# Output projection of a hybrid decoder layer: 512-column chunks of two k-tiles, three matmuls per stationary block

## The reference

```
h = h + jnp.einsum('btd,de->bte', merged, w_out[layer])
return rmsnorm(h, final_norm_w)
```

## Time and profile before

| | |
|---|---|
| median of three runs | 2974.49 us (2974.31 to 2974.5) |
| span of the profiled execution | 2972.4 us; the page states no other time for it |
| TensorE matmul, weight load | busy 2954.2 and 2585.2 us |
| VectorE, ScalarE | busy 1700.5 and 1311.9 us |
| DMA | 552.28 MB, 186 GB/s, hardware queue at 59.9% of 16 engines |
| granted TensorE clock | 0.999 on average |

### The profile page before, as it was taken

The page is one execution under the profiler, slowest core; times in us unless marked ns, Lnnn a source line. Parts: engine busy times, 40 slices in busy tenths (PEclk is TensorE's granted clock), DMA queues, the critical chain, the costliest instruction groups (busy, mean ns, idle before and its releaser), DMA issues.

```text
span 2972.4 us, 46667 instructions
## 1 busy us (share of the span) xinstructions
PE 2954.2 (99%) x17061; PEld 2585.2 (87%) x17061; DVE 1700.5 (57%) x1973; ACT 1311.9 (44%) x1526; POOL 6.9 (0%) x23
## 2 busy tenths in 40 slices
PE   9999999999999999999999999999999999999998
PEld 7888888888888888888888888888888888888887
DVE  7666666666665555555555555555555555555555
ACT  6444444444444444444444444444444444444444
POOL 0000000000000000000000000000000000000000
PEclk9999999999999999999999999999999999999999
DMA  7555555555556555555566666666666666666665
GB/s 242 178 177 168 170 174 174 171 171 169 174 169 190 187 185 184 182 188 188 186 187 185 185 188 184 185 184 188 185 185 187 184 185 188 184 207 205 207 206 193
DMA packets 550941, 552.28 MB, mean 186 GB/s; under 512 B 17217, under 2 KB 547826, under 8 KB 550898
## 3 DMA queue, kind: packets, MB, share of 16 engines
q1 hardware_dynamic: 550898, 551.71, 59.9%
HBM read 547.45 MB, written 4.19 MB: 186 GB/s over the span
## 4 chain that ended last, share of the span: by engine, by line
PE 99%; DMA 0%; DVE 0%; ACT 0%; ACTq 0%; SPq 0%; issue 0%; DVEq 0%
PE PS L833 64%; PE PS L828 33%; PE SC L874 1%; DMA XS<-in_x 0%; PE SS L874 0%; PE OB L883 0%; PE OB L884 0%; PE SC L864 0%; PE OB L882 0%; PE SS L889 0%; PE PS L819 0%; PE SC L819 0%; PE OB L819 0%; DVE WS L481 0%; ACT U L327 0%; ACT H L453 0%
## 5 line engine op out<-in xcount | busy, mean ns | idle before, releaser
L833 PE MATMUL PS<-U,WS 128*128 128x512 f32 x5632 | 1982.3, 396 | 0.0
L481 DVE TENSOR_TENSOR WS<-RAW,WS 128x1024 fp32r<-128x1024 f32 x1024 | 1249.4, 1225 | 1177.2 <-ACT WS L309 1146.2
L309 ACT ACTIVATE WS<-RAW 128x1024 fp32r<-128x1024 f32 x1024 | 1084.0, 1060 | 1591.9 <-PE PS L833 1589.2
L828 PE MATMUL PS<-U,WS 128*128 128x256 f32 x5632 | 1574.7, 282 | 0.5 <-DVE WS L481 0.5
L833 PEld LDWEIGHTS PS<-U,WS 128*128 128x128 f32 x5632 | 1053.3, 188 | 245.0
L828 PEld LDWEIGHTS PS<-U,WS 128*128 128x128 f32 x5632 | 1061.8, 189 | 8.8 <-issue 0.8
L833 PE MATMUL PS<-WS,U 128*128 128x512 f32 x1536 | 533.5, 390 | 0.0
L828 PE MATMUL PS<-WS,U 128*128 128x256 f32 x1536 | 430.8, 283 | 0.0
L833 PE MATMUL PS<-Y,WS 128*128 128x512 f32 x1024 | 361.7, 397 | 0.0
L833 PEld LDWEIGHTS PS<-WS,U 128*128 128x128 f32 x1536 | 287.3, 188 | 58.3
L828 PEld LDWEIGHTS PS<-WS,U 128*128 128x128 f32 x1536 | 290.1, 189 | 2.6
(11 more groups left out here) (161 smaller groups left out, 631.9 us busy)
## 6 DMA issues: line engine op xcount, KB each, us to landing
RAW<-in_w_in SPq DMA_DIRECT2D x768, 512.0 KB, 3.7
RAW<-in_w_out SPq DMA_DIRECT2D x128, 512.0 KB, 3.8
RAW<-in_w_branch_a SPq DMA_DIRECT2D x64, 512.0 KB, 3.7
RAW<-in_w_branch_b SPq DMA_DIRECT2D x64, 512.0 KB, 3.8
XS<-in_x SPq DMA_DIRECT2D x8, 512.0 KB, 9.5
XR<-in_x SPq DMA_DIRECT2D x16, 256.0 KB, 4.0
out_dram<-H SPq DMA_DIRECT2D x8, 512.0 KB, 4.2
FW<-in_final_norm_w SPq DMA_DIRECT2D x16, 128.0 KB, 3.8
```

The costliest lines, as they stand in the source:

```text
L309: act.activation(WS[s][:, :, 0:GW], RAW[s][:, :, :], ACT.Copy).then_inc(hi_ready, 1)
L481: dve.tensor_tensor(WS[s][:, :, GW:2 * GW], RAW[s][:, :, :], WS[s][:, :, 0:GW], ALU.subtract).then_inc(lo_ready, 1)
L828: return pe.matmul(bank[:, T:2 * T], stat_lo, both[:, 0:T], start=False, stop=stop, skip_group_check=True)
L833: op = pe.matmul(bank, stat_hi, both, start=first, stop=last, skip_group_check=True)
```

## The change

The output projection is cut into eight groups of 512 output columns. A chunk is still 512 KB and still fills one ring slot, but holds two k-tiles of 512 columns (`wide` is the view of the same tile). A group has sixteen chunks. For each k-tile and each half of the positions there are three matmuls of 512 columns into one bank: high x high, high x low and low x high, all three onto the same columns. The bank then holds the finished sum, so that the copy to `SM` and the addition that joined two halves of a bank go. VectorE adds the residual straight from PSUM, over [128, 2, 512], and multiplies by the gain; ScalarE squares 512 columns per half. `GA` and `GB` become two halves of one tile `HG`, which holds the group's `h`. The loads of `XR` and `FW` are twice as wide and half as many. The last four chunks of the merge stage prefill the ring with the first chunks of the output projection, so they use the wide view too.

```diff
+OW = 2 * GW
+CO = 2 * CD
+NO = D // OW
-TURNS_OUT = 2 * CD // RING
+TURNS_OUT = 2 * CO // RING
...
+        def wide(tile):
+            return tile[:, :, :].rearrange("p (k h) c -> p k (h c)", h=2)
...
-            with sp.Fori(0, NG // 2) as i:
+            with sp.Fori(0, NO // 2) as i:
                 for n in range(2):
-                    col = column(i * 2 + n, 0)
-                    for c in range(CD):
-                        load(w_out[0], c, col, OUT_TURN + TURNS_OUT * i + (n * CD + c) // RING, c % RING)
+                    cols = bass.ds((i * 2 + n + 1) * OW - OW, OW)
+                    for c in range(CO):
+                        s = c % RING
+                        src = w_out[0][c * 2 * P:(c + 1) * 2 * P, cols]
+                        sp.wait_ge(lo_ready, RING * (OUT_TURN + TURNS_OUT * i + (n * CO + c) // RING) + s - (RING - 1))
+                        sp.dma_start(wide(RAW[s]), src.rearrange("(k p) c -> p k c", p=P)).then_inc(raw_loaded[s], 16)
...
-                    small_half(OUT_GROUP + 2 * i + n, RING * (OUT_TURN + TURNS_OUT * i) + CD * (n + 1), n)
-                    act.wait_ge(h_ready, 2 * i + n + 1)
+                    act.wait_ge(drained, OUT_GROUP + 2 * i + n + 1)
                     for b in range(2):
-                        act.activation(SM[n][:, b, :], (GA, GB)[n][:, b * T:(b + 1) * T], ACT.Square,
+                        act.activation(SM[b][:, :, :], pair(HG[:, b, :]), ACT.Square,
                                        accum_out=SSQ[:, b, bass.ds(i * 2 + n, 1)]).then_inc(h_sq, 1)
...
-                    drain_group(h, OUT_GROUP + 2 * i + n, n)
-                    dve.tensor_tensor(h, h, XR[:, :, cols], ALU.add).then_inc(h_ready, 1)
+                    dve.wait_ge(w_used, RING * (OUT_TURN + TURNS_OUT * i) + CO * (n + 1))
+                    dve.wait_ge(xr_loaded[n], i * 32 + 32)
+                    if not (first and n == 0):
+                        dve.wait_ge(h_sq, 4 * i + 2 * n)
+                    dve.tensor_tensor(HG[:, :, :], PS[n][:, :, :], XR[:, :, cols], ALU.add).then_inc(drained, 1)
...
-                dve.tensor_tensor(small, PS[1][:, b, T:2 * T], XR[:, b, cols], ALU.add)
-                dve.tensor_tensor(h, PS[1][:, b, 0:T], small, ALU.add)
+                dve.tensor_tensor(h, PS[1][:, b, :], XR[:, b, cols], ALU.add)
...
+            def wide_chunk(par, c, halves=(0, 1)):
+                w = wide(WS[c % RING])
+                for k in range(2):
+                    at_k = 2 * c + k
+                    for b in halves:
+                        top, low = U[:, at_k, b * P:(b + 1) * P], U[:, at_k, T + b * P:T + (b + 1) * P]
+                        bank = PS[par][:, b, :]
+                        pe.matmul(bank, top, w[:, k, 0:OW], start=at_k == 0, stop=False)
+                        pe.matmul(bank, top, w[:, k, OW:2 * OW], start=False, stop=False)
+                        op = pe.matmul(bank, low, w[:, k, 0:OW], start=False, stop=at_k == KT - 1)
+                return op
...
+            for c in range(CO - RING):
+                pe.wait_ge(lo_ready, chunk0 + c + 1)
+                wide_chunk(1, c).then_inc(w_used, 1)
             for b in range(2):
-                for c in range(CD):
+                for c in range(CO - RING, CO):
```

More of the change, by code:

```diff
@@ L397, in merge @@
                 for c in range(2 * CD + 2 * CB):
-                    hi(turn + c // RING, c % RING)
+                    hi(turn + c // RING, c % RING, is_wide=last and c >= 2 * CD + 2 * CB - RING)
                     if c in (CD + 2, 2 * CD + 2):
@@ L430, in output @@
                 for n in range(2):
-                    for c in range(CD if not (last and n == 1) else RING):
-                        hi(OUT_TURN + TURNS_OUT * i + (n * CD + c) // RING + 1, c % RING)
+                    for c in range(CO if not (last and n == 1) else CO - RING):
+                        hi(OUT_TURN + TURNS_OUT * i + (n * CO + c) // RING + 1, c % RING, is_wide=True)
                     if last and n == 1:
@@ L728, in merge @@
                 for c in range(2 * CD + 2 * CB):
-                    lo(turn + c // RING, c % RING)
+                    lo(turn + c // RING, c % RING, is_wide=last and c >= 2 * CD + 2 * CB - RING)
                     if c == CD - 1:
@@ L756, in output @@
                 for n in range(2):
-                    for c in range(CD if not (last and n == 1) else RING):
-                        lo(OUT_TURN + TURNS_OUT * i + (n * CD + c) // RING + 1, c % RING)
+                    for c in range(CO if not (last and n == 1) else CO - RING):
+                        lo(OUT_TURN + TURNS_OUT * i + (n * CO + c) // RING + 1, c % RING, is_wide=True)
                     if last and n == 1:
                         break
-                    h = pair((GA, GB)[n])
@@ L771, in output @@
-                    dve.tensor_tensor(H[:, :, cols], h, fw, ALU.mult)
             output(0, first=True)
-            with dve.Fori(1, NG // 2 - 1) as i:
+            with dve.Fori(1, NO // 2 - 1) as i:
                 output(i)
[L776 to L781, removed]
+            output(NO // 2 - 1, last=True)
+            dve.wait_ge(h_sq, 2 * NO - 2)
+            dve.wait_ge(xr_loaded[1], NO // 2 * 32)
@@ L938, in output @@
             def output(i, first=False, last=False):
                 for n in range(1 if last else 2):
-                    group(OUT_TURN + TURNS_OUT * i, n * CD, CD, positions, U, 0, n, OUT_GROUP + 2 * i + n,
-                          u_wait=(m_ready, 1) if first and n == 0 else None)
+                    pe.wait_ge(drained, OUT_GROUP + 2 * i + n - 1)
+                    for c in range(CO):
+                        if first and n == 0 and c % 2 == 0:
+                            pe.wait_ge(m_ready, c // 2 + 1)
+                        at_chunk = n * CO + c
+                        pe.wait_ge(lo_ready, RING * (OUT_TURN + TURNS_OUT * i) + at_chunk + 1)
+                        wide_chunk(n, c).then_inc(w_used, 1)
```

59 lines of the change are left out of this document (30 added, 29 removed).

## The result

The changed kernel takes 2978.72 us (median of 20 runs, 2977.57 to 2983.5) against 2975.03 (20 runs, 2974.31 to 2976.16): ratio 1.0014, 95% interval 1.0008 to 1.002. It is slower by about 3.7 us, where 4.1 us less were forecast; the time lies 2.7 us above the top of the range.

What follows compares the result with a forecast made beforehand. TensorE's matmul stream was taken as the bound: 4.4 us saved in the output projection plus 0.3 us at the end gave -4.1 us, so 2974.5 becomes 2970.4 us, range 2967.5 to 2976.

Steps and rivals of the forecast that it cites:

- The bound: Whole kernel and output projection: TensorE busy 2954.2 of 2972.4 us, so a stage lasts as long as its matmuls follow one another.
- the middle, 228.4: Output projection: distance between 512-column matmuls taken as 228.4 ns, a triple 685.2 ns against 693.8 for two pairs, saving 4.4 us.
- about 13 ns a matmul: Output projection: cost beyond the columns, 26.9 ns of a 346.9 ns pair; if fixed, 512 fewer matmuls save 6.9 us.
- the 512-column stream is slower in the new pattern: Rival, output projection: 512s slower than 228.4 ns, a loss from 231.3 on; 2979.0 us at 234, 2988.2 at 240; chance 0.10.
- The cost goes with the columns: Rival, output projection: cost beyond the columns grows with them, stage 355.2 us, only the end remains, 2974.8 us; chance 0.05.
- The second load of the same block costs nothing: Rival, output-projection triples: array keeps the block, second matmul takes 213.3 ns, 7.7 us more saved, 2962.6 us; chance 0.07.
- The ring: Chunk supply at group ends: ScalarE back at +5.2 us, low part at +7.5, cover 3.5 us; rival wait 2977.4 us, chance 0.04.
- the end: Behind the last matmul: longer additions, squares and gain multiply on VectorE and ScalarE add 0.3 us.
- the other engines: VectorE, ScalarE and DMA inside the output stage: fewer but longer pieces, none on the path, costing only if they delay the ring.
- Half 0: Half 0's chain at the end: VectorE's idle time before half 1 shrinks from 0.48 us to 0.1 us.

Runs made afterwards that it cites:

- e3: Changed kernel with every 512-column matmul cut into two of 256 columns on the same stationary block; output stage 357.8 us, 116.7 ns a matmul.
- e4: Changed kernel with top x low as two 256-column matmuls, order 512, 256, 512, 256; 2975.3 us against 2975.28, ratio 1.0001.
- e7: Changed kernel with top x low in two halves, order 512, 512, 256, 256; 693.3 ns for the four matmuls.
- e1: Kernel before with the second matmul of each output-projection pair streaming all 512 columns; 477.6 us for 2047 distances, 233.3 ns a matmul.
- e2: Changed kernel with the second and third matmul of each triple exchanged; 357.7 us for 511 triples.
- e19: Kernel before with WS 96 bytes beyond U and Y modulo 128, output-projection activations in a tile 64 bytes beyond U; 2944.08 us, ratio 0.9895.
- e14: Changed kernel with 64 unused bytes a partition ahead of RAW and WS; 2945.78 us.
- e16: Kernel before with 64 unused bytes a partition ahead of RAW and WS; 2945.40 us.
- e18: Changed kernel with WS 96 bytes beyond U and Y modulo 128, output-projection activations in a tile 32 bytes beyond U; 2947.94 us, ratio 0.9908.
- e8: Changed kernel with 32 unused bytes a partition ahead of RAW and WS; 2982.58 us, 228.9 ns a matmul in the output stage.
- e15: Kernel before with 32 unused bytes a partition ahead of RAW and WS; 2988.58 us, 351.6 ns a pair in the output stage.

## Why the prediction was wrong

- **The bound** was read rightly: TensorE without waits before and after, and the stage as long as its matmuls follow one another.
- **The failed step** is this one: "The chain's 227 and this 230 are the two readings of the same thing; I take the middle, 228.4." Both came from 512s with 256s around them. In a stream of 512s alone the distance is 233.3 ns, 4.9 more, and 1536 x 4.9 = 7.5 us is the miss of the stage: +3.1 in place of -4.4. With the whole times, 3.7 against -4.1, it is 7.8. The 230 was also weaker than it was used: the row's 0.46 us allows 225 to 235, as the prediction says itself, yet further down it becomes "at most" 230. The trace's starts, to the nanosecond, put the next matmul 228 ns behind the last 512 of a group and 235 behind the first 512 of the next group, 231.5 on average. That is past the 231.3 from which the change loses.
- **Under it lay** "about 13 ns a matmul". 26.9 ns beyond the columns divided by two matmuls is arithmetic, not a measurement. e3 has twice the matmuls of the changed kernel in the same time, e4 the old number with a third more than it in 3.3 us less. What exceeds the columns depends on the mix of sizes and on the places of the tiles.
- **The rival "the 512-column stream is slower in the new pattern"** held: from 231.3 ns on, 2979.0 at 234, and 2978.72 was measured. It had 0.10. What spoke for it was in the rows: the branches' 234 ns, the same instruction slower. I set it aside because the same two tiles met; they meet at other sizes. Its reason, a top block loaded during a 512-column stream, is refuted: e7 has that in one of its two 512s and keeps the fast step, and e1 (half of the slots) and the changed kernel (two of three) have the same 233.3.
- **"The cost goes with the columns"** had 0.05 and 2974.8. Among uniform streams of 256 and 512 it is right (e3); it missed that the mixed stream is cheaper at this place, so it gave no loss.
- **"The second load of the same block costs nothing"**: refuted, loads equal matmuls (16549), and e2 takes the same time without reuse.
- The Trainium skill ("TensorE: Matmul & The Clock Gate", section "Back-to-back issue gap") gives N / 2.4 + 2.5 ns, 215.8 for 512 columns, and calls it the isolated gap of one matmul; for a stream of loads and matmuls the same section has about 131 ns at 512 columns. The prediction took the first for a stream. No run here comes near either: 228.9 to 233.3. The measurement decides for this kernel's fp32r operands.
- **The ring, the end, the other engines** came out as worked out: 0.3 us up to L807 (though not up to the last instruction), 4.8 and 7.1 us in the ring against 5.2 and 7.5. Half 0 left VectorE idle for 0.23 us where 0.1 was expected.

## What to carry to other kernels

A distance between matmuls read from one pattern of sizes doesn't hold for another: where TensorE is the bound, run the new pattern once, at full length, before reckoning with it. When the same instruction shows two distances at the same clock, look at where its two tiles start, and at what interrupted the stream last, before changing the algorithm: here 64 unused bytes were worth 29 us, eight times what the change cost. A row of 0.46 us is no evidence on a difference of 5 ns. And compare two shapes at several places, or a verdict on the shape is one on the allocator.

## What the runs showed of the hardware that was not expected

- At the full clock and without waits, 768 columns took from 343.3 to 351.6 ns in the output stage, by the start of two tiles and the mix of 512 and 256 columns. The columns alone would be 320 (estimate, from the prediction's 0.42 ns a column).
- The pairs ran at 347 ns wherever the stationary tile started 96 bytes beyond the moving one modulo 128: in the output stage of before and e19 (346.9, 346.7) and in the second branch and merge stage of e14, e16, e18 and e19 (346.7), which have the two tiles' roles exchanged. The converse does not hold: the first branch of the kernel before, at another place, had 346.7 too.
- One stream of pairs, with the same tiles and places, kept to 347 ns a pair or to 353, and went from one to the other at an interruption.
- A uniform stream of 256 columns (116.7 ns) costs half of one of 512 (233.3), but 384 cost 176.5. Mixing 512 and 256 saves 1% at the place of this case and costs 2% at the place of e8 and e15 (343.3 against 351.6).
- What in the reading of the two tiles collides is not shown here: no row names it. VectorE, ScalarE and DMA are not needed for the 233.3 ns, which stand with all of them idle (2957.5 to 2960.4 us).
